# Two more projections as seven block products: linear attention's queries and keys, differential attention's values

## The reference

```python
u = _rmsnorm(h, norm_g)
p = u @ w_in                    # 1024 -> dq dk dv gq gk gv gg gr
dq, dk, dv, gq, gk, gv, gg, gr = parts   # 512 512 512 256 256 512 512 16 columns
da = _diff_attention(dq[:, :, 0], dq[:, :, 1], dk[:, :, 0], dk[:, :, 1], dvh, lam)   # values: dv
qg = _split_heads(gq, GLA_HEADS).astype(f32) * (GLA_K_DIM ** -0.5)
kg = _split_heads(gk, GLA_HEADS).astype(f32)
log_a = _split_heads(jax.nn.log_sigmoid(gr @ gate_w + gate_b) / GLA_TAU, GLA_HEADS)
og = _gla_chunked(qg, kg, vg, log_a)     # linear attention, chunks of 64
gla_out = _merge_heads(_rmsnorm(og, gla_on)) * jax.nn.silu(gg)
return jnp.concatenate([da_out, gla_out], axis=-1) @ w_o
```

## Time and profile before

| what | value |
|---|---|
| median of 3 runs | 1098.99 us (1097.87 to 1099.45) |
| the profiled execution | 1098.47 us |
| its span in the trace | 1096.6 us |
| PE busy | 922.8 us (84%) |
| DVE busy | 403.1 us (37%) |
| POOL busy | 243.1 us (22%) |
| ACT busy | 167.2 us (15%) |

### The profile page before, as it was taken

The page is one execution under the profiler, slowest core; times in us unless marked ns, Lnnn a source line. Parts: engine busy times, 40 slices in busy tenths (PEclk is TensorE's granted clock), DMA queues, the critical chain, the costliest instruction groups (busy, mean ns, idle before and its releaser), DMA issues.

```text
span 1096.6 us, 12500 instructions
## 1 busy us (share of the span) xinstructions
PE 922.8 (84%) x5007; PEld 569.3 (52%) x5007; DVE 403.1 (37%) x995; ACT 167.2 (15%) x372; POOL 243.1 (22%) x366
## 2 busy tenths in 40 slices
PE   8999999999999999999999998666475566574757
PEld 4764487889999878864445653222222112131312
DVE  4647826762234737858445343010101001010101
ACT  2123223340001021013212230000000000000000
POOL 3534044053854949910000000000000000000000
PEclk9999999999999999999999998878778778787879
DMA  9545333223545254424439549999999999999996
GB/s 324 173 146 200 105 126 112 102 95 104 194 164 192 79 204 177 157 77 154 154 112 349 235 192 427 427 427 428 429 427 428 427 427 428 428 428 428 426 407 273
DMA packets 64344, 290.38 MB, mean 265 GB/s; under 512 B 9047, under 2 KB 11934, under 8 KB 51742
## 3 DMA queue, kind: packets, MB, share of 16 engines
q1 hardware_dynamic: 57856, 205.13, 48.8%
q10 hardware_dynamic: 6430, 84.44, 18.1%
HBM read 288.51 MB, written 1.05 MB: 264 GB/s over the span
## 4 chain that ended last, share of the span: by engine, by line
PE 62%; DMA 31%; DVE 5%; ACT 1%; issue 1%; SPq 0%; DVEq 0%; ACTq 0%
DMA ring<-in_w_e_up_dram 12%; PE ACC L539 12%; PE ACC L695 10%; DMA PJ<-in_w_e_up_dram 9%; DMA BIG<-in_w_e_up_dram 9%; PE ACC L554 9%; PE PAIR L1099 7%; PE ACC L692 7%; PE ACC L578 5%; PE ACC L990 3%; PE PAIR L589 2%; PE PAIR L666 1%; PE PAIR L643 1%; PE PAIR L724 1%; PE PAIR L1130 1%
## 5 line engine op out<-in xcount | busy, mean ns | idle before, releaser
L1351 POOL TENSOR_TENSOR ring<-ring 128x256 f32<-128x256 f32 x272 | 204.0, 781 | 165.1 <-PE ACC L692 75.6
L1099 PE MATMUL PAIR<-ring,R 128*32 128x512 f32 x400 | 132.0, 711 | 39.1 <-DMA BIG<-in_w_e_up_dram 19.7
L554 PE MATMUL ACC<-BIG,ring 128*128 128x256 f32 (+1 forms) x464 | 103.8, 381 | 0.6 <-DVE R L1938 0.6
L554 PEld LDWEIGHTS ACC<-BIG,ring 128*128 128x128 f32 (+1 forms) x464 | 85.4, 187 | 15.5 <-issue 3.1
L2402 DVE SCALAR_TENSOR_TENSOR GB<-GB,PAIR 128x512 f32<-128x512 f32 x8 | 5.5, 688 | 233.6 <-ACT GB L1745 233.6
L1099 PE MATMUL PAIR<-BIG,R 128*32 128x512 f32 x176 | 64.3, 740 | 20.9 <-DMA PJ<-in_w_e_up_dram 20.9
L1099 PE MATMUL PAIR<-R 128*32 128x512 f32 x176 | 60.0, 702 | 25.5 <-issue 13.0
L539 PE MATMUL ACC<-ring,BIG 128*128 128x512 f32 (+2 forms) x192 | 78.1, 559 | 0.5 <-DVE R L2238 0.5
L1130 PE MATMUL PAIR<-ring,BIG 128*32 128x512 f32 x160 | 63.4, 734 | 17.7 <-DMA R<-in_w_e_down_dram 13.0
L1099 PE MATMUL PAIR<-SQE,R 128*32 128x512 f32 x112 | 63.1, 728 | 17.6 <-DMA ring<-in_w_e_up_dram 11.0
L1099 PEld LDWEIGHTS PAIR<-ring,R 128*32 128x32 f32 x400 | 31.0, 128 | 72.8 <-issue 72.8
(11 more groups left out here) (351 smaller groups left out, 1400.3 us busy)
## 6 DMA issues: line engine op xcount, KB each, us to landing
ring<-in_w_in_dram SPq DMA_DIRECT2D x20, 2048.0 KB, 7.9
ring<-in_w_e_gate_dram SPq DMA_DIRECT2D x8, 2048.0 KB, 39.5
ring<-in_w_e_up_dram SPq DMA_DIRECT2D x6, 2048.0 KB, 41.5
ring<-in_w_e_gate_dram ACTq DMA_DIRECT2D x6, 2048.0 KB, 25.4
ring<-in_w_e_down_dram SPq DMA_DIRECT2D x5, 2048.0 KB, 39.3
ring<-in_w_e_up_dram ACTq DMA_DIRECT2D x5, 2048.0 KB, 21.0
ring<-in_w_ckv_dram SPq DMA_DIRECT2D x4, 2048.0 KB, 8.0
BIG<-in_w_e_down_dram SPq DMA_DIRECT2D x4, 2048.0 KB, 23.2
```

What stands on the lines that cost most here:

```text
L554: mm = nc.tensor.matmul(bank[0:m, j * S:(j + 1) * S], w[:, i, a + j * P:a + j * P + m], rhs[:, i, :], start=(i == 0), stop=(i == k - 1))
L1099: mm = nc.tensor.matmul(bank[r, :], M_xt[:, k, r], w[e][:, k, :], start=(k == 0), stop=(k == KD - 1))
L1351: ins = g.tensor_tensor(out[:, k, :], a[:, k, :], b[:, k, :], op)
```

## The change

`gqk` and `dv` are made by `project_blocks`, `gqk` turned. Both join the list of chunks that get weight sums; POOL makes the first three sums of `gqk` before its two memsets and the last behind them, and those of `dv` behind `QN`. `combine` of `gqk` stands on DVE behind `row_sums`, and writes GQ and GK; ACT then only scales GQ in place. `make_states` comes behind product 1 of `dv`, `finish_gla` behind product 3. ACT's drain of `dv` is gone. DVE combines parts 0 and 1 of `dv` before it gates `GG`, and parts 2 and 3 behind it, ahead of lambda and of `norm_heads`. `WS` is now free for its weight chunk (`wo1`) behind `dv` and not behind `gg`.

```diff
@@ -186,7 +186,7 @@
 
 
         gate_chunks = [f"gate{n}{h}" for n in range(3) for h in range(2)]
-        block_chunks = ["mv", "qi", "qm"] + gate_chunks + ["wout0", "wout1", "ckv0", "dq", "dk", "gv", "ckv1", "gg"]
+        block_chunks = ["mv", "qi", "qm"] + gate_chunks + ["wout0", "wout1", "ckv0", "gqk", "dq", "dk", "gv", "ckv1", "gg", "dv"]
         WS = slots[RING - 1]
         S_a, S_b = (WS[:, 1024 * i:1024 + 1024 * i].rearrange("p (k n) -> p k n", k=4) for i in range(2))
         T_x, T_mem2 = (t.rearrange("p (i k q) -> p i k q", i=4, k=4) for t in (WS[:, 2048:4096], R5[:, 2048:4096]))
@@ -860,7 +860,7 @@
             project_blocks("ckv0", R2T, T_mem2, mem2_sums, after=lambda done: turn_rows("x1", 1) if done == 20 else None)
             wait_turned("x1")
             project_t("gr", XT3, tiles=1, m=16)
-            project_t("gqk", XT3)
+            project_blocks("gqk", XT3, T_x, x1_sums, turned=True)
             wait_drained(pe, "gr")
             bank, full = acc("gate_z")
             for h in range(2):
@@ -925,7 +925,8 @@
                                                       skip_group_check=True)
                     mm.then_inc(full, 1)
 
-            project("dv", XT3, between=finish_gla, after=lambda done, total: make_states() if done == 4 else None)
+            project_blocks("dv", XT3, T_x, x1_sums,
+                           after=lambda done: make_states() if done == 8 else finish_gla() if done == 16 else None)
             for t in range(TT):
                 wait_drained(pe, ("dq", t))
                 wait_drained(pe, ("dk", t))
@@ -1352,7 +1353,7 @@
                 ins.then_inc(counter, 1)
                 pool.wait_ge(counter, value)
 
-            def weight_sums(name):
+            def first_sums(name):
 
                 c = block_chunks.index(name)
                 pool.wait_ge(slot_landed[slot_no[chunk_at[name]]], landed_value[chunk_at[name]])
@@ -1363,8 +1364,16 @@
                 add_steps(S_a, w21, w22, ALU.add, w_sums, 4 * c + 1)
                 add_steps(S_b, S_a, w11, ALU.subtract, w_sums, 4 * c + 2)
                 add_steps(w21, w11, w21, ALU.subtract, w_sums, 4 * c + 3)
+
+            def last_sum(name):
+                c = block_chunks.index(name)
+                w12 = slot_of(name)[:, 4:8, 0:256]
                 pool.wait_ge(block_products, 3 * c + 1)
                 add_steps(w12, w12, S_b, ALU.subtract, w_sums, 4 * c + 4)
+
+            def weight_sums(name):
+                first_sums(name)
+                last_sum(name)
 
             weight_sums("mv")
             for t in range(TT):
@@ -1413,10 +1422,12 @@
             g.memset(causal[0:64, 192:256], NEG).then_inc(pads_cleared, 1)
             for name in gate_chunks[3:6] + ["wout0", "wout1", "ckv0"]:
                 weight_sums(name)
+            first_sums("gqk")
             wait_full(pool, ("x1", 1, 1))
             wait_full(pool, ("x1", 1, 0))
             g.memset(ZT[:, :], 0.0).then_inc(pads_cleared, 1)
             g.memset(KEN, 0.0).then_inc(pads_cleared, 1)
+            last_sum("gqk")
             for name in ("dq", "dk"):
                 weight_sums(name)
 
@@ -1427,6 +1438,7 @@
             g.tensor_tensor(KE, kt(GK, 2), kt(EE, 2), ALU.mult).then_inc(gla_ends, 1)
             g.tensor_tensor(QP, kt(GQ, 2), kt(EP, 2), ALU.mult)
             g.tensor_tensor(QN, kt(GQ, 2), kt(EN, 2), ALU.mult).then_inc(gla_products, 1)
+            weight_sums("dv")
 
             for t in range(TT):
                 wait_full(pool, ("mix", t, 0))
@@ -1637,9 +1649,8 @@
 
             scale_mem2("ckv0", R1v, 0)
             drain("gr", [(GRT[:, :], lambda b: b[0:16, 0:S])])
-            bank = wait_full(act, "gqk")
-            a_.activation(GQ, bank[:, 0:512], ACT.Copy, scale=64 ** -0.5)
-            a_.activation(GK, bank[:, 512:1024], ACT.Copy).then_inc(free_sem("gqk"), 1)
+            wait_drained(act, "gqk")
+            a_.activation(GQ, GQ, ACT.Copy, scale=64 ** -0.5)
 
             bank = wait_full(act, "gate_z")
             for h in range(2):
@@ -1675,7 +1686,6 @@
             wait_drained(act, ("gla", 1))
             wait_drained(act, ("gla", 0))
             square_heads(OG, SQ[:, 0:1024].rearrange("p (t n) -> p t n", t=TT), 128)
-            drain("dv", by_token(DV, 0))
             soften("DA", 0, 9)
             act.wait_ge(gla_products, 1)
             act.wait_ge(gla_padded, 1)
@@ -2181,6 +2191,11 @@
             rsqrt(2, SMALL[:, 64:66], SMALL[:, 78:80]).then_inc(mem2_scaled, 1)
             row_sums(T_x, quarters(XT3), x1_sums)
 
+            def combine_gqk(parts):
+                gqk = R3[:, 1024:2048].rearrange("p (i j t q) -> p i j t q", i=2, j=2, t=TT)
+                combine("gqk", [gqk[:, i, :, t, :] for i in range(2) for t in range(TT)], parts)
+
+            combine_gqk(range(4))
             lam = GB[:, GB_LAM:GB_LAM + 256].rearrange("p (a b d) -> p a b d", a=2, b=2)
             link(v.tensor_tensor(lam[:, :, 0, :], lam[:, :, 0, :], lam[:, :, 1, :], ALU.mult))
             v.tensor_reduce(SMALL[:, 48:50], lam[:, :, 0, :], AX_X, ALU.add).then_inc(lambda_dots, 1)
@@ -2250,9 +2265,11 @@
                                                          scalar=DEC[r, 4 * h + c:4 * h + c + 1], in1=u_, op0=ALU.mult, op1=ALU.add)
                 ins.then_inc(free_sem(("state", c)), 1)
                 wait_drained(dve, ("state", c))
+            combine("dv", by_rows(DV), range(2))
             dve.wait_ge(tanh_ready, 4)
             link(v.scalar_tensor_tensor(out=GG, in0=R3[:, 0:1024].rearrange("p (t n) -> p t n", t=TT), scalar=1.0, in1=GG,
                                         op0=ALU.add, op1=ALU.mult))
+            combine("dv", by_rows(DV), range(2, 4))
             dve.wait_ge(lambda_exp, 1)
             link(v.tensor_tensor(SMALL[:, 53:54], SMALL[:, 51:52], SMALL[:, 50:51], ALU.subtract))
             link(v.tensor_scalar(SMALL[:, 54:55], SMALL[:, 53:54], -LAM_INIT, None, ALU.add))
```

## The result

| | before | after |
|---|---|---|
| median, 5 runs each | 1098.45 us | 1102.77 us |
| lowest to highest | 1097.63 to 1099.45 | 1101.69 to 1104.45 |
| span of the profiled execution | 1096.6 us | 1100.0 us |

The changed kernel is slower: ratio 1.0039, 95% interval 1.0029 to 1.0050, so 3.2 to 5.5 us. The forecast was 1102.0 us, 3.0 us slower. In the two profiles the span grows by 3.4 us. The profiled execution of the change took 1101.69 us and is the fastest of its five.

A forecast was written before the change was run, and what follows sets the result against it. PE was taken to bound the kernel almost throughout; `mask_scores` late +2.85, a DVE wait won back -0.26 and the clock +0.4 made +3.0 us, on the median 1098.99 a forecast of 1102.0 us, range 1098.0 to 1105.0.

The forecast's parts named there:

- `gqk` on PE: Block products of `gqk` take 1.3 us less and a 0.21 us wait for ACT goes; `dq` starts 1.55 us earlier.
- `gqk` on POOL: Sixteen more adds, mostly hidden in 9.08 us of POOL idle; its later train of adds starts 1.7 us earlier.
- The start of `dv`: Following POOL and PE, `dv` starts at 472.8 us in place of 474.51.
- `dv` on PE: Block form of `dv` saves 1.7 us: 21.2 us in place of 22.87, unhindered by POOL's new sums.
- The wait on DVE: Part 3 of `dv`'s combine delays the norm; first `mask_scores` 2.85 us later, PE stops 5.4 us before second scores.
- The clock: After PE's stop in `ckv3` its clock may fall to half speed: 0.4 us lost, bounds 0 and 1.5.
- The sum: Whole kernel: +2.85 - 0.26 + 0.4 = +3.0 us.
- The rival of a gain: PE's 3.2 us saved on `gqk` and `dv` arrive at the end, giving 1095.8 us; chance 0.13.

The follow-up runs named there:

- e1: Kernel before with only `gqk` as block products, `dv` plain and drained by ACT: 1097.10 us, ratio 0.9986 to before.
- e2: Kernel before with only `dv` as block products, `gqk` plain: 1104.59 us, ratio 1.0056 to before.
- e3: Changed kernel with parts 2 and 3 of `dv`'s combine inside the norm, behind its reduction and root: 1098.63 us, ratio 1.0004 to before.
- e4: Changed kernel with 24 needless bf16 matmuls keeping PE busy during its stop: 1101.43 us, ratio 1.0029 to before.
- e7: Changed kernel, norm's reduction and root ahead of parts 2 and 3, scaling and `GG * OG` behind attention, transposes at end of `ckv3`: 1096.27 us, ratio 0.9979 to before.
- e5: Changed kernel with attention ahead of the whole norm of `OG` on DVE, its transposes at the end of `ckv3`: 1099.23 us, ratio 0.9997 to before.
- e6: Kernel before with only DVE's reordering, attention ahead of the whole norm of `OG`: 1103.11 us, ratio 1.0029 to before.

## Why the prediction was right, point by point

- **`gqk` on PE.** Forecast: `dq` 1.55 us earlier. Measured 1.59, once the 0.39 us with which this profile came in are taken off. The turned form took 12.70 us to `gate_z`, 0.2 more than the two gate projections had shown; the wait for ACT is gone.
- **`gqk` on POOL.** Forecast: hidden by the idle 9 us. It was. The memsets came at 392.86 (forecast 393.6). One wait I had not named: `dq`'s first sum had to wait 0.86 us for product 3 of `gqk`, which still reads `S_b`. It cost nothing, for the next wait, for product 1 of `dq`, was the binding one, as forecast. (POOL's 9.08 us of idle begin behind the memsets, at 388.06, and not at 383.84 as that passage reads; its sum counts them right.) The train started 1.17 us earlier, 1.56 net of the 0.39; forecast 1.7.
- **The start of `dv`.** Forecast 472.8; measured 473.30, or 472.9 without the 0.39. PE's wait in `gg` came in two pieces, 0.55 us for DVE before it and 0.28 for the third sum, in place of 0.92.
- **`dv` on PE.** Forecast 21.2 us; measured 494.41 - 473.30 = 21.1. The new sums on POOL (11.37 us) were far ahead of their use.
- **The wait on DVE.** Forecast: norm at 494.95, `mask_scores` at 502.55, PE's stop 5.4 us. Measured 495.36, 502.84, 5.49, the first two late by 0.4 and 0.3, as the profile was from its start. e1, e2 and e3 show that this is the cause: without `dv`'s combine there is no loss, with it alone the whole, and with its last parts moved the loss goes.
- **The clock.** Forecast 0.4 us within 0 to 1.5; 0.7 by e4. In e2's profile the same kind of stop cost 1.8, so the upper bound was too low for some executions.
- **The sum.** Forecast +3.0, in three terms: +2.85, -0.26 and +0.4. The traces, without the 0.39 us: `mask_scores` +2.74; from there to the rest of `ckv3` 25.82 us before and 25.45 with the clock held up (e4), so -0.37; the clock +0.71. That is +3.1, and as much at `wo`, so mechanism and sizes hold in this profile. The timed median gives +4.3, with 3.2 as its lower end. The profiled execution (1101.69 us) is 1.1 us below that median, and what the other four spent more is not traced. Two things vary by as much: the price of the clock behind the stop (0.7 and 1.8 us, above), and the stretch from `wo` to the end, which no edit touches and which took 558.3 to 561.8 us in the ten profiles. Part of the nearness of 1102.0 to 1102.77 is luck: the forecast started from 1098.99, and the median of before in the comparison is 1098.45.
- **The rival of a gain** needed `mask_scores` not to bind. e7 makes that true, and 2.6 us of the 3.2 arrive (`wo` 2.57 us earlier, 2.8 from `gr` on).

## What to carry over

A drain that becomes a combine moves work from one engine's queue to another's. Ask what stands behind it in that queue, not how long it takes: parts 2 and 3 are 1.7 us of work and their place cost 3.5 us at `wo` (541.04 against 537.49 in e3), because they made an unrelated norm wait for the end of a projection. An instruction that waits for the newest result belongs behind all that is ready earlier, up to the point where its own consumer needs it; e5 and e6 show the other side, that work pushed behind attention must still be done before the next stage asks for it.

## What the runs showed of the hardware

Beside POOL's adds some of DVE's smallest operations take longer. In the root of the norm ahead of `row_sums`, an operation on two elements a partition took 0.16 to 0.17 us before, when POOL was idle; after, beside POOL's adds, five of the first seven took 0.56 to 0.65:

```profile
389.31 0.65 DVE L1795 TENSOR_SCALAR NWI<-NW 128x2 int32<-128x2 int32 x1
...
390.80 0.65 DVE L1806 SCALAR_TENSOR_TENSOR NW<-NW 128x2 f32<-128x2 f32 x1
...
393.05 0.16 DVE L1811 SCALAR_TENSOR_TENSOR NW<-NW 128x2 f32<-128x2 f32 x1
393.71 0.69 DVE L1962 TENSOR_TENSOR ring<-BIG 128x512 f32<-128x512 f32 x1
```

They are quick again from 392.85, when the memset begins. Without `gqk`'s sums (e2) all of them took 0.16 to 0.17, and with `gqk` alone (e1) five were slow again. `row_sums` (L1962) started at 393.71 for this, 2.7 us later than before, 0.4 of it from the profile's late start. That was not in the forecast, and cost nothing by luck: the first row sum was ready at about 394.4, and product 2 of `gqk` first reads it at 396.10. Operations of `combine`, which read PSUM, took 0.42 us with POOL busy (412.69) and idle (494.52) alike. The Trainium skill ("GPSIMD Engine Reference", "Specifications") says that POOL and DVE share SBUF interfaces and that DVE instructions in a two-port mode or with two SBUF inputs contend; the slow operations with two SBUF inputs fit it. Of two TENSOR_SCALARs, with one input each, the one at 389.31 took 0.65 and the one at 390.00 only 0.17; no run here shows which mode they ran in, so these stay open.
